# Layer-by-layer transformer trunk on one core: where the norms' sums are made and read, and in what order the mixer's small matmuls run

## The chip, the cores and the metric

One core of one Trainium2 chip runs the whole program in one launch. The metric is device microseconds (us) of one execution, the median over several. Engines are named as in the profile: PE is TensorE, PEld its weight loads, DVE VectorE, ACT ScalarE, POOL GpSimd, SP SyncE (which issues the loads).

## What is computed

```python
def reference(x, ...):                     # x: (1, 256, 1024) float32, DEPTH = 2
    for l in range(DEPTH):
        x = x + 0.5 * swiglu(rmsnorm(x, ffn1_norm[l]), ...)       # 1024 -> 2816 -> 1024
        x = x + hybrid_mixer(rmsnorm(x, mix_norm[l]), ...)
        x = x + 0.5 * swiglu(rmsnorm(x, ffn2_norm[l]), ...)
    return rmsnorm(x, final_norm)

def hybrid_mixer(h, ...):
    q_a, k_a, v_a, q_g, k_g, v_g, gate_lr, r_g = split(h @ w_in)
    attn = rmsnorm(sliding_window_attention(q_a, k_a, v_a, sinks), attn_out_norm)
    log_a = log_sigmoid(gate_lr @ gate_up + bias) / 16
    o = gla_chunked(q_g, k_g, v_g, log_a)                         # 4 chunks of 64 tokens
    gla = rmsnorm(o, gla_out_norm) * silu(r_g)
    return concat(attn, gla) @ w_out
```

The window is 128 tokens, 8 query heads share 2 key heads of 64, and the gated linear attention (GLA) has 4 heads with keys of 64 and values of 128. All weights are float32 in HBM and are read once.

## The kernel before

Activations lie transposed in SBUF: `resid` holds x as 8 tiles (k) of 128 features by 256 tokens. A float32 product is made of three fast `fp32r` matmuls: ACT rounds a weight unit to `whi` (L756), DVE makes `wlo = raw - whi` (L977), x is split in the same way into `xhi` (ACT, L770) and `xlo` (DVE, L982), and PE adds whi*xhi, whi*xlo and wlo*xhi (`three`, L358 to L360). A weight unit is 1 MB at most and goes through one of three slots (`raw`, `whi`, `wlo`); SP may load a slot again when `lo_done` tells that DVE has split it. A layer is 81 units: 33 of FFN 1, 15 of the mixer, 33 of FFN 2. Inside an FFN a hardware loop runs over groups of three units (gate, up, down); its hidden parts lie in `h_parts`.

The mixer's units are, in the order of the slots, KV, V1, Q0, Q1, QG, KG, V0, R0, R1 and six of `w_out` (`WO_K`: k = 0, 1, 2 and 3, 4, 5, 6 and 7). Units KV to R1 are projections of the normed x; k 0 to 3 of the output projection read the attention output, 4 to 7 the GLA output. Between the projections stand small float32 matmuls, each of which shows as two records on PE (a transpose as one): the scores of the 8 heads (L521), the transposes of the probabilities S (`turn_probs`, L534) and of `kend` (L587), the GLA's intra-chunk products (L604, called A here), the attention's product with V (L622 to L626), the state updates (L641), and the GLA output (L664 from A, L668 from the states `Sta`).

A norm is a seam. The last unit of a stage leaves its sum in four PSUM banks (`acc`); DVE adds them to `resid` one after the other (L1004), ACT makes `xhi` and squares `resid` (L772), POOL adds the squares up in four steps into `sqsum` (`sum_squares`, L1346), PE sums over the partitions with two matmuls against `ones` (`square_sums`, L407), and DVE works out 1/sqrt by twelve steps on two columns (`rsqrt`, L1022 to L1029). The factor is wanted along the tokens: DVE makes diagonal matrices of it in two `fp32r` parts (`diagonals`, L1034 to L1039, in `h_parts`), PE spreads them over the partitions (`spread`, L415), and DVE copies the result to `rB` (L1050). Meanwhile PE goes on with matmuls on the unnormed x, since the factor is multiplied in when a PSUM tile is read. At the seam into the mixer PE runs `up_pairs` for unit KV, `square_sums`, then unit V1, then Q0 with `spread` after its first half. At the seams into an FFN `square_sums` stands one tile later. The attention's norm and the GLA's norm go the same way with `sqsum_a` (L650, POOL too) and with 8 columns (L706).

The order of the work is that of the program text: each engine's stream is written out by hand in its own block and waits on semaphores with fixed counts. ACT's and DVE's `split_mix(i)` split unit i.

## Time and profile before

| | us |
|---|---|
| median of 3 runs | 1011.42 |
| the three runs | 1007.83, 1011.63, 1011.42 |
| the profiled execution | 1007.62 |
| its span, from the first to the last instruction | 1005.7 |
| PE busy | 972.5 (97%) |
| DVE busy | 628.4 (62%) |
| ACT busy | 457.2 (45%) |
| POOL busy | 55.8 (6%) |

The page gives busy times as a share of the span. A matmul's record is longer than the distance to the next one, since they are pipelined, so a PE that is busy all the time says only that matmuls followed one another closely; how closely is read from the number of records in a stretch. The granted clock (PEclk) is a share of 2.4 GHz; it has two levels here, 1.0 and 0.5. Layer 0 runs to about 499 us, with its mixer from 200 to 309 us; layer 1's mixer runs from 691 to 803 us.

### The profile page before, as it was taken

To read this page: it belongs to the slowest core of one execution; us is meant where nothing else is said; L and a number is where in the kernel's file an instruction comes from. 1 tells how busy PE (TensorE), PEld (TensorE's weight loads), DVE (VectorE), ACT (ScalarE), POOL (GpSimd) and SP (SyncE) were. 2 spreads that over 40 slices of the span, in tenths; PEclk is the share of its full clock that TensorE was granted. 3 is DMA by queue.
4 is the path that set the end of the run, shared out by engine and by line. 5 is a ranking of instruction groups with operands and counts; after the bars stand their busy time and mean duration, and the time that the engine had idled before them with its cause. 6 is when DMAs were issued, how large, how long until landed. Compare 5 with 4: busy or idle time off the path is not lost.

```text
span 1005.7 us, 20058 instructions
## 1 busy us (share of the span) xinstructions
PE 972.5 (97%) x8116; PEld 959.1 (95%) x8116; DVE 628.4 (62%) x743; ACT 457.2 (45%) x499; POOL 55.8 (6%) x37
## 2 busy tenths in 40 slices
PE   7999999989999999999979999998999999999996
PEld 6999999989999999999979999998998999999996
DVE  7755555667778655555665555557595785555553
ACT  5443434536645443434534343435475544343432
POOL 4000000030101000000120000003001010000000
PEclk8999999989999999999999999999998999999997
DMA  7665656544335665655446556555442556565621
GB/s 259 219 207 169 206 169 209 169 127 126 85 98 197 211 199 174 193 183 185 149 137 218 197 177 198 177 200 155 140 105 63 170 167 210 168 199 175 190 102 43
DMA packets 130621, 169.13 MB, mean 168 GB/s; under 512 B 3217, under 2 KB 116113, under 8 KB 130577
## 3 DMA queue, kind: packets, MB, share of 16 engines
q1 hardware_dynamic: 130576, 168.52, 53.0%
q8 instruction: 31, 0.51, 0.2%
q14 instruction: 14, 0.11, 0.0%
HBM read 167.46 MB, written 1.05 MB: 168 GB/s over the span
## 4 chain that ended last, share of the span: by engine, by line
PE 77%; issue 14%; DVE 4%; POOL 3%; DMA 1%; ACT 1%; SPq 0%; DVEq 0%; ACTq 0%; POOLq 0%
PE ps L358 25%; PE ps L359 25%; PE ps L360 25%; POOL sq L1346 2%; DVE xlo L982 2%; PE ps L668 1%; DVE wlo L977 1%; PE ps L664 1%; DMA raw<-in_ffn_w_gate 1%; DMA raw<-in_ffn_w_up 1%; ACT xhi L770 0%; PE ps L415 0%; POOL sqsum_a L1346 0%; PE ps L738 0%; PE ps L706 0%
## 5 line engine op out<-in xcount | busy, mean ns | idle before, releaser
L977 DVE TENSOR_TENSOR wlo<-raw,whi 128x2048 fp32r<-128x2048 f32 (+1 forms) x159 | 355.6, 2239 | 249.5 <-ACT whi L756 249.5
L358 PE MATMUL ps<-xhi,whi 128*128 128x256 f32 x1760 | 498.7, 283 | 12.8 <-DVE wlo L977 6.1
L359 PE MATMUL ps<-xlo,whi 128*128 128x256 f32 x1760 | 494.5, 281 | 0.0
L360 PE MATMUL ps<-xhi,wlo 128*128 128x256 f32 x1760 | 493.8, 281 | 0.0
L756 ACT ACTIVATE whi<-raw 128x2048 fp32r<-128x2048 f32 (+1 forms) x159 | 297.2, 1869 | 182.7 <-PE ps L360 168.9
L358 PEld LDWEIGHTS ps<-xhi,whi 128*128 128x128 f32 x1760 | 333.6, 190 | 17.2 <-issue 7.1
L359 PEld LDWEIGHTS ps<-xlo,whi 128*128 128x128 f32 x1760 | 333.0, 189 | 0.1
L360 PEld LDWEIGHTS ps<-xhi,wlo 128*128 128x128 f32 x1760 | 332.9, 189 | 0.0
L359 PE MATMUL ps<-h_parts,whi 128*128 128x256 f32 x704 | 196.1, 279 | 0.0
L360 PE MATMUL ps<-h_parts,wlo 128*128 128x256 f32 x704 | 196.1, 278 | 0.0
L358 PE MATMUL ps<-h_parts,whi 128*128 128x256 f32 x704 | 196.0, 278 | 0.0
L360 PEld LDWEIGHTS ps<-h_parts,wlo 128*128 128x128 f32 x704 | 133.6, 190 | 0.0
L358 PEld LDWEIGHTS ps<-h_parts,whi 128*128 128x128 f32 x704 | 132.2, 188 | 0.0
L359 PEld LDWEIGHTS ps<-h_parts,whi 128*128 128x128 f32 x704 | 132.1, 188 | 0.0
L1346 POOL TENSOR_TENSOR sq<-sq 128x512 f32<-128x512 f32 x21 | 42.5, 2025 | 928.6 <-ACT sq L772 625.8
L784 ACT ACTIVATE h_parts<-work 128x512 fp32r<-128x512 f32 x44 | 27.8, 632 | 145.3 <-DVE work L1066 85.0
L777 ACT ACTIVATE work<-work 128x512 f32<-128x512 f32 x44 | 27.8, 633 | 133.8 <-DVE work L1058 133.8
L1070 DVE TENSOR_TENSOR h_parts<-work,h_parts 128x512 fp32r<-128x512 f32 x44 | 30.4, 692 | 30.8 <-ACT h_parts L784 30.8
L1063 DVE TENSOR_TENSOR work<-ps,rB 128x512 f32<-128x512 f32 x44 | 30.1, 684 | 3.2 <-PE ps L360 3.2
L1066 DVE TENSOR_TENSOR work<-work 128x512 f32<-128x512 f32 x44 | 30.5, 692 | 2.1 <-ACT work L777 0.7
L1058 DVE TENSOR_TENSOR work<-ps,rB 128x512 f32<-128x512 f32 x44 | 30.2, 686 | 0.3
L982 DVE SCALAR_TENSOR_TENSOR xlo<-resid,par,xhi 128x256 fp32r<-128x256 f32 x40 | 27.6, 739 | 0.0
(138 smaller groups left out, 525.7 us busy)
## 6 DMA issues: line engine op xcount, KB each, us to landing
raw<-in_ffn_w_down SPq DMA_DIRECT2D x44, 1024.0 KB, 4.9
raw<-in_ffn_w_up SPq DMA_DIRECT2D x43, 1024.0 KB, 5.4
raw<-in_ffn_w_gate SPq DMA_DIRECT2D x42, 1024.0 KB, 5.4
raw<-in_w_in SPq DMA_DIRECT2D x12, 1024.0 KB, 5.2
raw<-in_w_in SPq DMA_DIRECT2D x8, 512.0 KB, 4.5
...
```

The source lines that it names most:

```text
L358: pe.matmul(o, w_hi, x_hi, start=start, stop=False, skip_group_check=True)
L359: pe.matmul(o, w_hi, x_lo, start=False, stop=False, skip_group_check=True)
L360: return pe.matmul(o, w_lo, x_hi, start=False, stop=stop, skip_group_check=True)
L756: nc.scalar.activation(h, r, ACT.Copy).then_inc(hi_done, 1)
L777: nc.scalar.activation(s32[:, :, :], a32[:, :, :], ACT.Silu).then_inc(silu_done, 1)
L977: nc.vector.tensor_tensor(lo, r, h.bitcast(F32), ALU.subtract).then_inc(lo_done, 1)
L982: nc.vector.scalar_tensor_tensor(out=xlo[:, m, :], in0=resid[:, m, :], scalar=gain[:, m:m + 1], in1=xhi[:, m, :].bitcast(F32), op0=ALU.mul ...
L1058: nc.vector.tensor_tensor(a32[:, :, :], tiles(bank), r_tiles(2), ALU.mult).then_inc(a_done, 1)
L1063: nc.vector.tensor_tensor(u32[:, :, :], tiles(bank), r_tiles(2), ALU.mult).then_inc(u_done, 1)
L1066: nc.vector.tensor_tensor(h32[:, :, :], s32[:, :, :], u32[:, :, :], ALU.mult).then_inc(h_done, 1)
L1070: nc.vector.tensor_tensor(hlo[hb][:, :, :], h32[:, :, :], hhi[hb][:, :, :].bitcast(F32), ALU.subtract).then_inc(hlo_done, 1)
L1346: return nc.gpsimd.tensor_tensor(o, a, b, ALU.add)
```

## The change

Of the norms: the squares are made by two ACT instructions of four tiles each (`squares`), after the next unit's split and no longer between the `xhi` of the seam; DVE adds them up in three instructions (`sum_squares`), POOL keeps the program's first and last sum alone; the mixer's `square_sums` stands after the first token tile of V1. `diagonals` is gone at all places: `spread` is now float32 matmuls of the factor's column, broadcast, against the identity, which wait for the last step of `rsqrt`; in the mixer it stands before Q0. DVE adds the attention's squares too.

Of the mixer's order: the gate's small matmuls go before Q1; each set of scores goes one projection earlier; the A products stand together ahead of the `kend` transposes and of all eight heads' transposes; R0 goes from before these to behind the state updates; in the GLA output all eight products with A come first, then the twelve with the states, in pairs of heads; the GLA's square sums stand inside R1 and its `spread` after the second `w_out` unit. The split attention output (k 0 to 3) goes to `h_parts` instead of `xhi` and `xlo`, since R1 still reads those. ACT and DVE have their splits and evictions in a new order to match.

The diff's core (declarations of semaphores and buffers, and copies that only change place, are left out, and every line stands 8 columns to the left):

```diff
+at_parts = h_parts[:, :, :, :].rearrange("p (a b) f t -> p a (b f) t", a=2)
+mixhi = [at_parts[:, 0, k, :] for k in range(4)] + [xhi[:, k, :] for k in range(4, KT)]
+mixlo = [at_parts[:, 1, k, :] for k in range(4)] + [xlo[:, k, :] for k in range(4, KT)]
...
-    def spread(o, n, a, b):
-        for part in range(2):
-            d = diag[:, part * n + a:part * n + b, :].rearrange("p a b -> p (a b)")
-            last = pe.matmul(o, ones_r[:, :], d, start=part == 0, stop=part == 1, skip_group_check=True)
+    def spread(o, call, y, n):
+        pe.wait_ge(rs_step, RS * (call + 1))
+        for i in range(n):
+            last = pe.matmul(o[i // 4][:, i % 4 * P:(i % 4 + 1) * P], y[:, i:i + 1].to_broadcast([P, P]), ident,
+                             start=True, stop=True, skip_group_check=True)
         return last
...
+    def project_tokens(i, t, outs, between=None):
...
+            if tt == 0 and between:
+                between()
...
-        square_sums(v)
-        project_tokens(M_V1, t, [ps[1][:, 0:WIDE], ps[2][:, 0:WIDE]])
+        project_tokens(M_V1, t, [ps[1][:, 0:WIDE], ps[2][:, 0:WIDE]], lambda: square_sums(v))
         pe.wait_ge(resid_up, 4 * (v + 1))
-        project(M_Q0, t, tiles(7), lambda: spread_r(v))
-        pe.wait_ge(rb_done, v + 1)
-        pe.wait_ge(lr_tok_ev, 2 * ev)
-        for tt in range(TT):
-            last = pe.transpose(ps[3][0:RANK, tt * P:(tt + 1) * P], lr_tok[:, tt, :], ident)
-        last.then_inc(lr_ps, 1)
+        spread_r(5 * l + 1, rcol)
+        def rank_tokens():
+            pe.wait_ge(rb_done, v + 1)
+            pe.wait_ge(lr_tok_ev, 2 * ev)
+            for tt in range(TT):
+                last = pe.transpose(ps[3][0:RANK, tt * P:(tt + 1) * P], lr_tok[:, tt, :], ident)
+            last.then_inc(lr_ps, 1)
+        project(M_Q0, t, tiles(7), rank_tokens)
...
+        pe.wait_ge(va_ev, ev)
+        pe.wait_ge(z_ev, 2 * ev)
+        pe.wait_ge(ke_done, ev)
+        pe.wait_ge(qe_done, ev)
+        for j in range(2):
+            for tt in range(TT):
+                for h in (2 * j, 2 * j + 1):
+                    b, c = DK * (h % 2), (2 * j + tt) * P
+                    last = pe.matmul(ps[3 + h % 2][:, c:c + P], ke[b:b + DK, j, tt * P:(tt + 1) * P],
+                                     qe[b:b + DK, j, tt * P:(tt + 1) * P],
+                                     start=True, stop=True, skip_group_check=True)
+                    if j == 1 and tt == TT - 1:
+                        last.then_inc(A_ps, 1)
         pe.wait_ge(qg_ev, ev)
-        project(M_R0, t, tiles(1))
-        pe.wait_ge(z_ev, 2 * ev)
         pe.wait_ge(kend_done, ev)
         for j in range(2):
             for tt in range(TT):
-                last = pe.transpose(ps[4][:, (2 * j + tt) * P:(2 * j + tt + 1) * P],
+                last = pe.transpose(ps[1][:, (2 * j + tt) * P:(2 * j + tt + 1) * P],
                                     kend[:, j, tt * P:(tt + 1) * P], ident)
         last.then_inc(ket_ps, 1)
...
-        for s in range(3):
+        for s in range(HEADS):
             turn_probs(s, l)
-        pe.wait_ge(ke_done, ev)
...
-                last.then_inc(A_ps, 1)
-            if h:
...
-            turn_probs(s, l)
...
+        pe.wait_ge(ket_ev, ev)
...
-        project(M_R1, t, tiles(0), attention_sums)
+        project(M_R0, t, tiles(0), attention_sums)
+        def o_tile(h):
+            return tiles(1 + h % 2)[:, h // 2, :]
+        pe.wait_ge(kg_ev, ev)
+        for h in range(GH):
+            j = h // 2
+            for tt in range(TT):
+                pe.matmul(o_tile(h)[:, tt * P:(tt + 1) * P], vg[:, tt, h * P:(h + 1) * P],
+                          AT[:, 4 * (h % 2) + 2 * j + tt, :],
+                          start=(h < 2 and tt == 0), stop=False, skip_group_check=True)
+        spread([ps[3][:, 256:512]], 5 * l + 2, rs_y, TT).then_inc(rA_ps, 1)
+        pe.wait_ge(st_done, 5 * ev)
+        for j in range(2):
+            for c in range(1, NCH):
+                for h in (2 * j, 2 * j + 1):
+                    b = DK * (h % 2)
+                    last = pe.matmul(o_tile(h)[:, c * CHUNK:(c + 1) * CHUNK], Sta[b:b + DK, c - 1, j, :],
+                                     qe[b:b + DK, j, c * CHUNK:(c + 1) * CHUNK],
+                                     start=False, stop=True, skip_group_check=True)
...
+                    if j == 1 and c == NCH - 1:
+                        last.then_inc(o_ps, 1)
+        def gla_sums():
+            pe.wait_ge(am_done, 4 * l + 2)
+            pe.wait_ge(osq_done, 2 * ev)
+            for h in range(GH):
+                for tt in range(TT):
+                    last = pe.matmul(ps[3][:, 2 * h + tt:2 * h + tt + 1],
+                                     sq[:, 4 + h, tt * P:(tt + 1) * P], ones[:, 0:1],
+                                     start=True, stop=True, skip_group_check=True)
+            last.then_inc(oss_done, 1)
...
         pe.wait_ge(rg_ev, 2 * l + 1)
-        pe.wait_ge(kg_ev, ev)
...
-        pe.wait_ge(st_done, 5 * ev)
-        for h in range(GH):
-            j, b = h // 2, DK * (h % 2)
...
-            o = tiles(1 + h % 2)[:, h // 2, :]
-            for tt in range(TT):
-                pe.matmul(o[:, tt * P:(tt + 1) * P], vg[:, tt, h * P:(h + 1) * P], AT[:, 4 * (h % 2) + 2 * j + tt, :],
-                          start=(h < 2 and tt == 0), stop=False, skip_group_check=True)
-                for c in (2 * tt, 2 * tt + 1):
-                    if c:
-                        last = pe.matmul(o[:, c * CHUNK:(c + 1) * CHUNK], Sta[b:b + DK, c - 1, j, :],
-                                         qe[b:b + DK, j, c * CHUNK:(c + 1) * CHUNK],
-                                         start=False, stop=True, skip_group_check=True)
-            if h >= 2:
-                last.then_inc(o_ps, 1)
...
-            if h == 0:
-                pe.wait_ge(adiag_done, ev)
-                spread(ps[3][:, 256:512], TT, 0, TT).then_inc(rA_ps, 1)
+        project(M_R1, t, tiles(0), gla_sums)
...
                 for m in range(KT):
                     w_hi, w_lo = weights(slot, n, D, m * P, P)
-                    last = three(acc[m // 2][:, m % 2, :], w_hi, w_lo, xhi[:, k, :], xlo[:, k, :],
+                    last = three(acc[m // 2][:, m % 2, :], w_hi, w_lo, mixhi[k], mixlo[k],
...
-                if k == 2:
-                    pe.wait_ge(o_ev, 2 * ev)
-                    pe.wait_ge(odiag_done, ev)
-                    for b in range(2):
-                        r = spread(ps[1 + b][:, :], 8, 4 * b, 4 * b + 4)
...
             last.then_inc(unit_done, 1)
...
+            if i == M_WO + 1:
+                pe.wait_ge(o_ev, 2 * ev)
+                spread([ps[1], ps[2]], 5 * l + 3, rs_y, 8).then_inc(rG_ps, 1)
...
-            nc.scalar.activation(sq[:, 2 * p:2 * p + 2, :], resid[:, 2 * p:2 * p + 2, :],
-                                 ACT.Square).then_inc(sq_done, 1)
+    def squares():
+        for half in range(2):
+            four = slice(4 * half, 4 * half + 4)
+            nc.scalar.activation(sq[:, four, :], resid[:, four, :], ACT.Square).then_inc(sq_done, 1)
...
         split_mix(2)
+        squares()
         split_mix(3)
-        act.wait_ge(rcol_done, ev)
-        v_out(M_V1, [ps[1][:, 0:UC], ps[2][:, 0:UC]])
+        act.wait_ge(rs_step, RS * (5 * l + 2))
+        act.wait_ge(unit_done, ST + 3 * t + M_V1 + 1)
         for tt in range(TT):
             nc.scalar.activation(lr_tok[:, tt, :], ps[1 + tt][:, UC:WIDE], ACT.Copy,
                                  scale=rcol[:, tt:tt + 1]).then_inc(lr_tok_ev, 1)
+        v_out(M_V1, [ps[1][:, 0:UC], ps[2][:, 0:UC]])
...
+        for s in range(4):
+            probs_out(s)
+        act.wait_ge(ket_ps, ev)
+        nc.scalar.copy(ket[:, :, :].rearrange("p a b -> p (a b)"), ps[1][:, :]).then_inc(ket_ev, 1)
         v_out(M_V0, [ps[0][:, 0:UC], ps[0][:, UC:2 * UC]])
+        for s in range(4, HEADS):
+            probs_out(s)
         split_mix(9)
-        exps(1)
-        act.wait_ge(ket_ps, ev)
-        nc.scalar.copy(ket[:, :, :].rearrange("p a b -> p (a b)"), ps[4][:, :]).then_inc(ket_ev, 1)
-        for s in range(HEADS):
-            probs_out(s)
...
-        nc.vector.tensor_copy(rs_parts[:, 0:n], rs_y[:, 0:n]).then_inc(part_step, 1)
-        dve.wait_ge(part_step, 2 * call + 1)
-        nc.vector.tensor_tensor(rs_parts[:, n:2 * n], rs_y[:, 0:n], rs_parts[:, 0:n].bitcast(F32),
-                                ALU.subtract).then_inc(part_step, 1)
-        dve.wait_ge(part_step, 2 * call + 2)
-        return nc.vector.tensor_tensor(
-            diag[:, 0:2 * n, :], ident.unsqueeze(1).to_broadcast([P, 2 * n, P]),
-            rs_parts[:, 0:2 * n].bitcast(F32).unsqueeze(2).to_broadcast([P, 2 * n, P]), ALU.mult)
-    def norm_r(v, call):
+    def norm_r(v, call, y):
         dve.wait_ge(ss_done, v + 1)
-        rsqrt(call, ps[3][:, 0:TT], TT, D)
-        diagonals(call, TT).then_inc(diag_done, 1)
+        rsqrt(call, ps[3][:, 0:TT], TT, D, y[:, 0:TT])
+    def flat(a, b):
+        return sq[:, a:b, :].rearrange("p m t -> p (m t)")
+    def sum_squares(v, steps):
+        dve.wait_ge(sq_done, 2 * v)
+        nc.vector.tensor_tensor(flat(0, 4), flat(0, 4), flat(4, 8), ALU.add).then_inc(sum_step, 1)
+        dve.wait_ge(sum_step, steps + 1)
+        nc.vector.tensor_tensor(flat(0, 2), flat(0, 2), flat(2, 4), ALU.add).then_inc(sum_step, 1)
+        dve.wait_ge(sum_step, steps + 2)
+        nc.vector.tensor_tensor(sqsum[:, :], sq[:, 0, :], sq[:, 1, :], ALU.add).then_inc(sqsum_done, 1)
...
-        norm_r(v, 5 * l + 4 * f)
+        norm_r(v, 5 * l + 4 * f, rs_y)
         split_lo(0, t + 1)
...
+        sum_squares(v, 7 * l)
         split_mix(2)
-        norm_r(v, 5 * l + 1)
-        nc.vector.tensor_copy(rcol[:, :], rs_y[:, 0:TT]).then_inc(rcol_done, 1)
+        norm_r(v, 5 * l + 1, rcol)
         split_mix(3)
         norm_b(v)
         dve.wait_ge(rb_done, v + 1)
...
         normalised(0)
-        split_mix(9)
-        normalised(1)
         for b in range(2):
             dve.wait_ge(A_ps, 2 * l + b + 1)
             dve.sem_inc(waits_met, 1)
             nc.vector.copy_predicated(AT[:, 4 * b:4 * b + 4, :], mask.unsqueeze(1).to_broadcast([P, 4, P]),
                                       ps[3 + b][:, :].rearrange("p (a t) -> p a t", a=4)).then_inc(A_ev, 1)
-        done(M_R0)
-        nc.vector.tensor_tensor(sg[:, 0:2, :], tiles(1), r_tiles(2), ALU.mult).then_inc(rg_ev, 1)
+        normalised(1)
+        split_mix(8)
...
+        dve.wait_ge(asq_done, 2 * ev)
+        nc.vector.tensor_tensor(flat(0, 2), flat(0, 2), flat(2, 4), ALU.add).then_inc(sum_step, 1)
+        dve.wait_ge(sum_step, 7 * l + 3)
+        nc.vector.tensor_tensor(sqsum_a[:, :], sq[:, 0, :], sq[:, 1, :], ALU.add).then_inc(asum_done, 1)
+        split_mix(9)
         dve.wait_ge(ass_done, ev)
-        rsqrt(5 * l + 2, ps[3][:, 0:TT], TT, 512)
-        diagonals(5 * l + 2, TT).then_inc(adiag_done, 1)
-        done(M_R1)
-        nc.vector.tensor_tensor(sg[:, 2:4, :], tiles(0), r_tiles(2), ALU.mult).then_inc(rg_ev, 1)
+        rsqrt(5 * l + 2, ps[3][:, 0:TT], TT, 512, rs_y[:, 0:TT])
+        done(M_R0)
+        nc.vector.tensor_tensor(sg[:, 0:2, :], tiles(0), r_tiles(2), ALU.mult).then_inc(rg_ev, 1)
         dve.wait_ge(rA_ps, ev)
         for b in range(2):
...
+                sum_squares(3 * l + 3, 7 * l + 5)
                 split_lo(2, t0 + TURNS)
...
+        sum_squares(3 * l + 2, 7 * l + 3)
...
-    def sum_squares(v, steps):
-        pool.wait_ge(sq_done, 4 * v - 3)
-        for p in (1, 2, 3):
-            pool.wait_ge(sq_done, 4 * v - 3 + p)
-            add(flat(0, 2), flat(0, 2), flat(2 * p, 2 * p + 2)).then_inc(pool_step, 1)
-            pool.wait_ge(pool_step, steps + p)
-        add(sqsum[:, :], sq[:, 0, :], sq[:, 1, :]).then_inc(sqsum_done, 1)
```

At the seam into the mixer this is what DVE does after the last `xlo`. Before:

```order
117 L975 REGISTER_ALU
118 L977 TENSOR_TENSOR wlo<-raw,whi 128x2176 [waits hi_done]
119 L975 REGISTER_ALU
120 L977 TENSOR_TENSOR wlo<-raw,whi 128x2x16x64 [waits hi_done]
121 L1044 REGISTER_ALU
122 L1022 TENSOR_SCALAR rs_v<-ps 128x2 [waits ss_done]
```

And with the change:

```order
111 L980 TENSOR_TENSOR wlo<-raw,whi 128x2176 [waits hi_done]
112 L1045 REGISTER_ALU
113 L1046 TENSOR_TENSOR sq<-sq 128x1024 [waits sq_done]
114 L1047 ISA
115 L1048 TENSOR_TENSOR sq<-sq 128x512 [waits sum_step]
116 L1049 REGISTER_ALU
117 L1050 TENSOR_TENSOR sqsum<-sq 128x256 [waits sum_step]
118 L978 REGISTER_ALU
119 L980 TENSOR_TENSOR wlo<-raw,whi 128x2x16x64 [waits hi_done]
120 L1037 REGISTER_ALU
121 L1026 TENSOR_SCALAR rs_v<-ps 128x2 [waits ss_done]
```

Three additions stand between the split of V1 (2176 wide) and that of Q0, and the first of them waits for ACT's squares.

In PE's stream the GLA output began like this before (one row is one matmul):

```order
1002 L664 MATMUL ps<-AT,vg 128x128 [waits st_done]
1003 L668 MATMUL ps<-qe,Sta 128x64
1004 L664 MATMUL ps<-AT,vg 128x128
1005 L668 MATMUL ps<-qe,Sta 128x64 x2
1006 L415 MATMUL ps<-h_parts,ones_r 128x256 [waits adiag_done]
1007 L415 MATMUL ps<-h_parts,ones_r 128x256
```

And is this, whole, with the change:

```order
949 L659 MATMUL ps<-AT,vg 128x128 [waits kg_ev]
950 L659 MATMUL ps<-AT,vg 128x128 x7
951 L412 ISA
952 L414 MATMUL ps<-cst,rs_y 128x128 [waits rs_step]
953 L414 MATMUL ps<-cst,rs_y 128x128
954 L664 REGISTER_ALU
955 L669 MATMUL ps<-qe,Sta 128x64 [waits st_done]
956 L669 MATMUL ps<-qe,Sta 128x64 x11
```

The two kinds of product no longer alternate, and the wait for the states comes after the products that don't need them.

## Rows read from the trace of the kernel before

**Rows 1.** The page's first part: busy time, share and instructions of each engine.

```profile
PE 972.5 (97%) x8116; PEld 959.1 (95%) x8116; DVE 628.4 (62%) x743; ACT 457.2 (45%) x499; POOL 55.8 (6%) x37
```

**Rows 2.** PE's waits over the span: us in total, times, longest.

```profile
PE ps L407 <- POOL sqsum L1346: 10.1, 3, 4.5
...
PE ps L358 <- DVE wlo L977: 6.1, 4, 3.8
...
PE ps L650 <- POOL sqsum_a L1346: 1.0, 2, 0.5
```

**Rows 3.** Timeline of POOL at the first mixer seam: start, us, instruction, idle before.

```profile
203.71 6.09 POOL L1346 TENSOR_TENSOR sq<-sq 128x512 f32<-128x512 f32 x1 [1.05 <-ACT sq L772]
209.88 0.72 POOL L1346 TENSOR_TENSOR sqsum<-sq 128x256 f32<-128x256 f32 x1
```

**Rows 4.** Timeline of DVE: `xlo` at the seams into the mixer and FFN 2; layer 1's first splits.

```profile
202.02 2.11 DVE L982 SCALAR_TENSOR_TENSOR xlo<-resid,par,xhi 128x256 fp32r<-128x256 f32 x4
...
309.76 4.67 DVE L982 SCALAR_TENSOR_TENSOR xlo<-resid,par,xhi 128x256 fp32r<-128x256 f32 x4
...
502.34 4.48 DVE L977 TENSOR_TENSOR wlo<-raw,whi 128x2048 fp32r<-128x2048 f32 x2
```

**Rows 5.** Stretches: length, each engine's busy us (instructions), granted clock, DMA, GB/s.

```profile
210.65:216.49 5.84, 5.84 (x26) 5.84 (x27) 4.30 (x17) 0.00 (x0) 0.00 (x0) 0.50 0.66 210
259.64:268.26 8.62, 8.62 (x95) 7.38 (x93) 4.92 (x14) 5.87 (x16) 0.00 (x0) 1.00 0.30 82
276.26:283.52 7.26, 7.26 (x44) 5.75 (x42) 6.25 (x9) 4.91 (x6) 0.00 (x0) 1.00 0.01 3
308.95:325.81 16.86, 15.49 (x127) 14.81 (x126) 14.97 (x24) 8.36 (x10) 4.82 (x4) 1.00 0.44 145
498.46:520.52 22.06, 16.83 (x126) 16.21 (x125) 13.54 (x24) 9.39 (x11) 9.04 (x4) 0.92 0.48 153
...
772.86:779.69 6.83, 6.83 (x28) 6.15 (x28) 3.27 (x2) 2.44 (x4) 0.00 (x0) 0.50 0.46 154
38.43:43.88 5.45, 5.45 (x50) 5.45 (x49) 2.94 (x3) 2.44 (x2) 0.00 (x0) 1.00 0.80 286
340.20:345.80 5.60, 5.60 (x50) 5.60 (x49) 3.37 (x3) 2.44 (x2) 0.00 (x0) 1.00 0.59 190
```

**Rows 6.** Timeline of PE: small matmuls, and the start of layer 1.

```profile
259.64 0.60 PE L587 MATMUL ps<-cst,kend 128*128 128x128 f32 x4
260.08 1.15 PE L534 MATMUL ps<-cst,S 128*128 128x128 f32 x9
261.15 0.72 PE L604 MATMUL ps<-qe,ke 64*128 64x128 f32 x8
...
265.70 0.27 PE L626 MATMUL ps<-PT,va 128*64 128x128 f32 x1
...
267.84 0.27 PE L624 MATMUL ps<-PT,va 128*64 128x128 f32 x1
...
276.26 0.38 PE L664 MATMUL ps<-AT,vg 128*128 128x128 f32 x2
276.57 0.43 PE L668 MATMUL ps<-qe,Sta 64*128 64x64 f32 x2
...
516.07 0.38 PE L358 MATMUL ps<-xhi,whi 128*128 128x256 f32 x1 [3.81 <-DVE wlo L977]
```

**Rows 7.** Groups of one shape: count, busy us, mean ns, idle before.

```profile
L977 DVE TENSOR_TENSOR wlo<-raw,whi 128x1024 fp32r<-128x1024 f32 x8 | 9.8, 1219 | 0.0
L1027 DVE SCALAR_TENSOR_TENSOR rs_a<-rs_a,rs_v 128x2 f32<-128x2 f32 x27 | 4.3, 161 | 0.9
L1156 DVE TENSOR_TENSOR bd<-bb 128x256 f32<-128x256 f32 x4 | 1.5, 422 | 0.1
```

**Rows 8.** Timeline of ACT: the seam's last `xhi`, and the split behind it.

```profile
202.13 0.91 ACT L770 ACTIVATE xhi<-resid,par 128x256 fp32r<-128x256 f32 x2 [1.00 <-DVE resid L1004]
...
203.47 1.90 ACT L756 ACTIVATE whi<-raw 128x2048 fp32r<-128x2048 f32 x1
```

170 lines of the change are left out of this document (62 added, 108 removed).

## The prediction

> **What bounds the kernel now.** I read the page's first part, then PE's waits, then the stretches at the seams, then the timelines inside them. PE is busy for 972.5 us of a span of 1005.7 [rows 1], so the program is PE's stream of matmuls, and a change can only take away PE's waits, make the same matmuls follow one another faster, or undo half clock. PE's waits [rows 2] are few: 10.1 us for POOL's `sqsum` in three places (the longest 4.5, twice, at the mixer's seams, and 1.08 at the seam between the layers), 6.1 for DVE's `wlo` (3.8 of it at one place), 1.0 for `sqsum_a`. Everything on the other engines beside these is hidden.
>
> At the mixer's seam POOL's third addition (512 wide) takes 6.09 us, the 256 wide one behind it 0.72 [rows 3]. DVE's four `xlo` take 2.11 there, but 4.67 at FFN 2's seam [rows 4], where POOL is busy for 4.82 us [rows 5]. So POOL's and DVE's operations, both of which read two tensors of SBUF, hold each other up; alone, POOL's 512-wide one would be near twice 0.72.
>
> Behind the wait at the mixer's seam comes a stretch at half clock (granted 0.50): PE, at 1.2 instead of 2.4 GHz, works in it from 210.65 to 216.49 [rows 5], 5.84 us, half of which is lost, 2.92. A second cause is the small matmuls. The V products follow one another in 0.054 us (40 records from 265.70 to 267.84), since two tiles of 64 columns run at once; the four `kend` transposes on the whole array take 0.11 each (0.44 from 259.64 to 260.08) [rows 6]. The GLA output takes 7.26 us for 44 records [rows 5], 0.165 each, because it alternates two forms: from the first pair at 276.26 the next form starts 0.31 later [rows 6], where two records of one form take 0.22.
>
> **The change, part by part.** The sum is made against the profiled execution, 1007.6 (3.8 below the median of the runs, 1011.4; one half-clock stretch more costs about 3.4, see below, so I take the gap for that and do not add it).
>
> *The mixer's seam.* DVE gets three additions between V1's split and Q0's. A 1024-wide two-tensor operation takes 1.22, a 256-wide one 0.42 [rows 7], so 512 take 0.7 and the three 2.3. Working layer 0: ACT's last `xhi` ends at 203.0 before; without the squares between them it ends at 202.05. Then come a split of 1.90 [rows 8] to 203.95 and two squares of half that width, about 1.0 each, to 205.9. DVE's last `xlo` ends at 202.9, V1's split (2.3, as each of the two at 502.34 [rows 4]) at 205.2; DVE then waits for ACT, and adds until 208.3. Behind its wait stands Q0's split, done at 210.6, which PE wants at 212.5. PE runs `up_pairs` until 205.9, where it stops today, and V1's first tile (24 matmuls of 272 columns, 0.117 x 272 / 256 = 0.125 each) until 208.9. So the sums are there 0.6 before PE asks for them. The wait of 4.5 goes, and with it the half clock that follows it: 4.5 + 2.9 = 7.4 a layer, **-14.9** in two.
>
> *The seams into FFN 2 and between the layers.* In 308.95 to 325.81 PE needs 120 matmuls of 0.117 (5.60 for 48 in FFN 2) and 0.6 for the sums and the spread, 14.6 of 16.86 [rows 5]; 2.2 are waits, for POOL or for an `xlo` that POOL slows. I take 1.9 of it, **-3.8** in two. The Trainium skill ("SBUF — State Buffer", who interferes with whom) has a VectorE operation with two SBUF inputs and a GpSimd one that reads SBUF lock each other out for a whole instruction. By that rule the four `xlo` here would go back to 2.11 from 4.67, 2.6 a seam and no more than the waits allow, so the term would be -4.4 and the sum 983.4; without the rule, were `xlo` slow for a cause of its own, nothing would go here and the sum be 987.8. The trace agrees with the rule as far as 4.67 beside POOL and 2.11 ahead of it go. Between the layers (22.06 us [rows 5]) 3.81 [rows 6] are a wait that the profile puts down to `wlo`, though the splits of that unit ended at 506.8 [rows 4], 5.4 us before PE stopped; I read it as the turn of PE's outer loop, which stays with its half clock (0.92 on the mean of 22 us). What is left is the 1.1 for POOL and smaller ones: **-1.5**.
>
> *The GLA output.* Sixteen records of A products at 0.11 are 1.76; the spread's four 0.44; twelve state products in pairs of heads (64 rows each, side by side as the V products) 24 x 0.054 = 1.3; two changes of form 0.4. Together 3.95 for 7.26: **-6.6** in two layers. From below: if the pairs do not run side by side, 1.3 a layer are lost. In layer 1 this output stands in a stretch of 6.83 at clock 0.50 [rows 5], which costs 3.4; without the alternation I expect none: **-3.4**.
>
> *The attention's sums* are on DVE, behind the states, before R0 is half done, and R1's split behind them is needed a unit later, so the wait of 0.5 a layer [rows 2] goes: **-1.0**.
>
> *The transposes and A products.* The stretch 259.64 to 268.26 takes 8.62 [rows 5]. It loses four changes of form at 0.1 to 0.2, but the cover that R0 gave it is gone: the softmax of heads 3 to 7 has to be ready at V0's end. ACT's copies of P (8 of 384 columns; two of 256 take 0.91 [rows 8]) take 3.7 against 2.9 for the transposes (three at 0.12 a head), so PE waits for PSUM banks toward the end. I cost it at nothing, between -0.6 (only the changes of form) and +1.5 a layer (the 0.8, and as much for its hand-overs).
>
> *The float32 spreads.* Two fp32r matmuls of 256 columns become four records at 0.11 with two changes of form: 0.24 becomes 0.6, +0.35 at six seams, +2.1. The GLA's goes from four matmuls of 512 columns (0.24 each, twice a 256-wide one, 0.94 in all) to 16 records at 0.11 and a change of form, 1.9: +1.0 a layer, +2.0. Together **+4.1**. `diagonals` leaves DVE, three operations a norm, which were hidden behind Q0's first half or V1; with `spread` now before Q0, rsqrt is on the path instead.
>
> *New waits.* rsqrt is twelve steps of about 0.2 (0.161 busy [rows 7] and the semaphore): 2.35. DVE reaches it at 210.6, behind Q0's split, and ends at 212.95, where PE comes to `spread` at 212.5: 0.5 a layer. `gla_sums` in the middle of R1 waits for ACT's squares of the GLA output, which now start 10 us nearer to it: 0.35 a layer. Behind both stand only matmuls that nothing else is late for. Together **+1.7**. Some more changes of form in the mixer, **+0.4**, and for fourteen hand-overs between engines that I cannot see 0.1 each, **+1.4**.
>
> Sum: -14.9 - 3.8 - 1.5 - 6.6 - 3.4 - 1.0 + 4.1 + 1.7 + 0.4 + 1.4 = -23.6, so **984.0**. R0's new place adds no matmul, and SP's loads see the slots freed in the same order; at the seams they lead by several us (DMA busy 0.3 to 0.5 of these stretches [rows 5]).
>
> One thing nobody edited: 48 down matmuls of an FFN take 5.45 in FFN 1 and 5.60 in FFN 2 [rows 5]. The instructions are the same and only their place in the program differs, and that moves by some rows. Over 1056 such matmuls in the two FFN 2 (0.003 each) this is 3.3 us to win, or as many to lose in FFN 1. The forecast's own range goes down from 984.0 by that 3.3, by 1.4 (no hand-overs), 1.7 (no new waits), 1.2 (the transposes at their best) and 1.4 (a spread with no change of form), to 975, and up by 3.3, by 2.6 (pairs not side by side) and 3.0 (the transposes at their worst), to 993.
>
> **The rivals.** *The clock still falls.* Before, the same GLA output kept full clock in layer 0 and stood at half in layer 1 (772.86 to 779.69 [rows 5]), with the same instructions, so a fall is not decided by the program's text alone. One or two stretches at 3.4: 987.4 or 990.8. The Trainium skill ("TensorE: Matmul & The Clock Gate") has a clock gate that is not tied to the kernel's start; by that rule the place of a fall varies from run to run, which the trace bears out as far as two layers with one program differ. Against a fall: behind the seam PE no longer idles. Chance 0.14.
>
> *The sums come too late again.* The margin of 0.6 rests on ACT: a split of 1.90 and two squares between its last `xhi` and the additions [rows 8]. If ACT is 1.5 late, PE waits at V1's half, and the clock falls as before. The most is the whole of the first term back, 14.9: 998.9. Chance 0.10.
>
> *No change:* waits move (to rsqrt, to P's copies and to the late W splits) and the time stays within 0.5% of 1011.4, about what a measurement of this kernel can tell from none. The terms above would have to be refilled by 20 us, with only four new places to wait: 0.04.
>
> *Slower: PE's inner loop pays for its turn.* The outer loop's turn costs 3.81 [rows 6] with all data there. The mixer's code before FFN 2 grows shorter by 14 rows, so FFN 2's hardware loop lies elsewhere. If its turn came to cost the same, 18 passes (9 in each layer) would be 69 us, 1053; the change is slower from 9 of 18 passes on. No pass of an inner loop shows such a wait before. The Trainium skill ("Runtime: NRT & Kernel Launch", instruction fetch) has instructions fetched ahead in order, and a taken jump to one not held waits for its fetch; the 3.81 agrees, and no run here shows a wait of the inner loop. Chance 0.05.
>
> **How the numbers follow.** Forecast 0.67, clock 0.14, late sums 0.10, no change 0.04, slower 0.05. Faster by over 0.5% are the first three, 0.91. The range from 975 to 999 holds the forecast, the clock's cases and nearly all of the late sums.
>
> **What would show it.** Right: no PE wait for `sqsum`, granted clock 1.0 from 200 to 220 us, a GLA output of 4 us, POOL nearly idle and FFN 2's four `xlo` near 2.1. Wrong: a wait at L407's successor or at `spread` above 1 us, half clock in a mixer, transposes over 10 us from V0's end to the V products' end, or FFN 2's 48 down matmuls far from 5.6.

## The result, and the profile after

| | before | after |
|---|---|---|
| median, us | 1009.62 (4 runs) | 973.38 (4 runs) |
| lowest to highest | 1005.07 to 1011.63 | 971.09 to 977.13 |
| the profiled execution | 1007.62 | 971.30 |

The ratio is 0.9651, with a 95% interval of 0.9599 to 0.9703. The forecast was 984.0, with 975 to 999: the sign is right, the gain is larger than the range allowed.

The first two parts of the page of the kernel after (busy time by engine, and the granted clock in 40 slices):

```profile
PE 950.8 (98%) x8156; PEld 942.1 (97%) x8156; DVE 617.2 (64%) x729; ACT 456.6 (47%) x489; POOL 11.4 (1%) x13
...
PEclk9999999999999999999999999999999999999998
```

PE has 40 matmul records more than in [rows 1] and is busy 22 us less; POOL works only at the start and in the last norm. PE's waits over the span of the kernel after (us in total, times, longest):

```profile
PE ps L357 <- DVE wlo L996: 5.2, 2, 2.8
PE ps L414 <- DVE rs_y L1033: 2.4, 1, 2.4
PE ps L357 <- issue: 1.6, 1, 1.6
PE ps L535 <- ACT PT L875: 1.1, 2, 0.6
PE ps L716 <- DVE ones L1288: 1.1, 1, 1.1
PE ps L535 <- DVE S L1192: 0.6, 2, 0.3
PE ps L681 <- ACT sq L909: 0.5, 2, 0.3
PE ps L414 <- DVE rcol L1033: 0.4, 2, 0.2
```

Against [rows 2]: the 10.1 for `sqsum` and the 1.0 for `sqsum_a` are gone. New are four waits of the mixer: for ACT's copies of P (`PT`), for DVE's probabilities (`S`), for the GLA's squares and for the mixer's rsqrt (L414, `rcol`), 2.6 us in both layers together. The 3.8 at the start of layer 1 is now 1.6, and the profile puts it down to "issue": it shows nothing that PE waited for.

The stretches that answer to [rows 5] (start and end, length, busy us of PE, PEld, DVE, ACT, POOL with instructions, granted clock, DMA, GB/s):

```profile
201.20:213.67 12.47, 12.32 (x102) 12.10 (x100) 11.26 (x24) 6.96 (x8) 0.00 (x0) 1.00 0.39 113
248.02:257.02 9.00, 8.13 (x94) 6.79 (x93) 6.50 (x18) 7.60 (x21) 0.00 (x0) 1.00 0.02 2
264.36:268.17 3.81, 3.81 (x47) 3.62 (x45) 2.07 (x5) 3.44 (x4) 0.00 (x0) 1.00 0.15 61
...
485.59:502.01 16.42, 14.84 (x126) 14.64 (x125) 13.49 (x24) 10.34 (x11) 0.00 (x0) 1.00 0.45 150
...
37.25:42.90 5.65, 5.65 (x50) 5.65 (x49) 3.11 (x4) 2.44 (x2) 0.00 (x0) 1.00 0.79 278
323.93:329.38 5.45, 5.45 (x51) 5.45 (x50) 2.98 (x3) 2.40 (x2) 0.00 (x0) 1.00 0.81 286
```

They are: the seam into the mixer up to `spread` (12.5 at full clock); A products, transposes and V products (9.0, where it was 8.6); the GLA output (3.8, where it was 7.3); the seam between the layers (16.4, where 22.1 stood); and 48 down matmuls of layer 0, first of FFN 1 (5.65), then of FFN 2 (5.45). Before it was 5.45 and 5.60, the other way round. Below, "pace" means this: whether an FFN's 48 down matmuls take 5.45 or 5.65 us.

DVE at the mixer's seam and at FFN 2's, after (start, us, instruction, idle before):

```profile
203.60 2.41 DVE L980 TENSOR_TENSOR wlo<-raw,whi 128x2176 fp32r<-128x2176 f32 x1
206.77 1.23 DVE L1046 TENSOR_TENSOR sq<-sq 128x1024 f32<-128x1024 f32 x1 [0.76 <-ACT sq L771]
208.03 0.69 DVE L1048 TENSOR_TENSOR sq<-sq 128x512 f32<-128x512 f32 x1
208.75 0.42 DVE L1050 TENSOR_TENSOR sqsum<-sq 128x256 f32<-128x256 f32 x1
...
301.23 1.66 DVE L985 SCALAR_TENSOR_TENSOR xlo<-resid,par,xhi 128x256 fp32r<-128x256 f32 x4
```

The sums are there at 209.17, and PE asks at 209.88: 0.7 us to spare, where 0.6 was forecast. The four `xlo` take 1.66 where they took 4.67 beside POOL [rows 4].

Cut at the ends of the same FFN steps, the 36.3 us between the two profiled executions lie like this. From the start to the end of layer 0's FFN 1 +1.1; layer 0's mixer with the seams 140.1 to 128.2, -11.9; FFN 2 158.3 to 156.2, -2.1; the seam between the layers with the first step behind it 36.2 to 30.8, -5.4; layer 1's FFN 1 156.2 and 156.2; its mixer 143.4 to 128.2, -15.2; its FFN 2 158.3 to 156.2, -2.1; the end -0.7.

### The profile page after: what moved, and what is told of

Read it like the earlier page. It is cut to its first block, busy times and chain, and to the rows that moved or that the text cites. A ratio compares the mean times of both kernels' runs of the same rounds, so it can differ in the third digit from the quotient of the medians.

```text
span 969.5 us, 20036 instructions
## 1 busy us (share of the span) xinstructions
PE 950.8 (98%) x8156; PEld 942.1 (97%) x8156; DVE 617.2 (64%) x729; ACT 456.6 (47%) x489; POOL 11.4 (1%) x13
## 4 chain that ended last, share of the span: by engine, by line
issue 97%; DMA 1%; POOL 1%; PE 0%; DVE 0%; SPq 0%; POOLq 0%; DVEq 0%
DMA raw<-in_ffn_w_gate 1%; POOL sq L1349 0%; PE ps L736 0%; DVE sq L1341 0%; SPq L284 0%; POOLq L98 0%; SPq L287 0%; PE ps L414 0%; POOL sq L1358 0%; POOL sqsum L1349 0%; DVEq L98 0%; DVE rs_y L1033 0%; DVE rs_a L1031 0%; DVE rs_a L1030 0%; SPq L286 0%
## 5 line engine op out<-in xcount | busy, mean ns | idle before, releaser
L357 PE MATMUL ps<-xhi,whi 128*128 128x256 f32 x1696 | 477.2, 281 | 6.8 <-DVE wlo L996 5.2
L358 PE MATMUL ps<-xlo,whi 128*128 128x256 f32 x1696 | 475.0, 280 | 0.0
L359 PE MATMUL ps<-xhi,wlo 128*128 128x256 f32 x1696 | 474.0, 279 | 0.0
L357 PEld LDWEIGHTS ps<-xhi,whi 128*128 128x128 f32 x1696 | 319.3, 188 | 9.3 <-issue 5.4
L359 PEld LDWEIGHTS ps<-xhi,wlo 128*128 128x128 f32 x1696 | 318.4, 188 | 0.0
L357 PE MATMUL ps<-h_parts,whi 128*128 128x256 f32 x768 | 213.2, 278 | 0.0
L358 PE MATMUL ps<-h_parts,whi 128*128 128x256 f32 x768 | 213.1, 277 | 0.0
L359 PE MATMUL ps<-h_parts,wlo 128*128 128x256 f32 x768 | 213.0, 277 | 0.0
L357 PEld LDWEIGHTS ps<-h_parts,whi 128*128 128x128 f32 x768 | 144.2, 188 | 0.0
L358 PEld LDWEIGHTS ps<-h_parts,whi 128*128 128x128 f32 x768 | 144.1, 188 | 0.0
L1074 DVE TENSOR_TENSOR h_parts<-work,h_parts 128x512 fp32r<-128x512 f32 x44 | 30.4, 691 | 30.8 <-ACT h_parts L782 30.8
L1007 DVE SCALAR_TENSOR_TENSOR resid<-ps,resid 128x512 f32<-128x512 f32 x24 | 16.6, 690 | 11.5 <-PE ps L359 11.5
L764 ACT ACTIVATE xhi<-resid,par 128x256 fp32r<-128x256 f32 x40 | 18.2, 502 | 7.8 <-DVE resid L1007 7.7
```

The lines of the kernel that those rows point to most:

```text
L357: pe.matmul(o, w_hi, x_hi, start=start, stop=False, skip_group_check=True)
L358: pe.matmul(o, w_hi, x_lo, start=False, stop=False, skip_group_check=True)
L359: return pe.matmul(o, w_lo, x_hi, start=False, stop=stop, skip_group_check=True)
L764: nc.scalar.activation(xhi[:, m, :], resid[:, m, :], ACT.Copy, scale=gain[:, m:m + 1]).then_inc(xhi_done, 1)
L1074: nc.vector.tensor_tensor(hlo[hb][:, :, :], h32[:, :, :], hhi[hb][:, :, :].bitcast(F32), ALU.subtract).then_inc(hlo_done, 1)
```

## Experiments: what the sums are worth

The kernel before was timed again beside each group of runs: medians 1003.28 (first four), 1006.80 (next four) and 1006.56 (last three), of 13 runs each. Its runs reach from 996.5 to 1014.7, so the ratio, with its 95% interval behind it, and the traces say more than differences of medians.

**The new sums alone** (`before_new_sums`):

```diff
 # the kernel before
+    squares()                      # two of four tiles, after the next split; none between the xhi
...
+    sum_squares(v, 6 * l)          # on DVE, three additions, in place of POOL's four
...
-    square_sums(v)
-    project_tokens(M_V1, t, ...)
+    project_tokens(M_V1, t, ..., lambda: square_sums(v))
```

> The kernel before with one part of the change alone: squares in two instructions after the next split, the norms' sums on DVE, and in the mixer read after V1's first tile; the order of the mixer's small matmuls, the fp32r spreads and the attention's sums on POOL stay. Theory A (the sums are nearly all of it): 24 to 27 us less than before, 976 to 982 where before is 1003 to 1007, and the order of the mixer is worth 5 to 8 us. Rival B (the parts share one gain, the clock): under 18 us less. At the turn of the loop between the layers: 3.8 us idle as before, if that idle time follows from where the code lies; 1.6 or less, if it came from the wait for the sums ahead of it.

984.64 (982.33 to 987.70), ratio 0.9803 (0.9729 to 0.9878), profiled 983.92: 23.7 less than the profiled execution before, but 22.2 less by the medians and 19.8 by the ratio. That is between the two theories, nearer to A; the interval of the ratio (12 to 27 us) can't choose. PE's waits of this run:

```profile
PE ps L359 <- issue: 2.1, 1, 2.1
...
PE ps L652 <- POOL sqsum_a L1368: 1.0, 2, 0.5
PE ps L416 <- DVE h_parts L1047: 0.9, 1, 0.9
```

No wait for `sqsum` is left. The turn of the loop (PE's jump from the end of layer 0 back to the start of the loop's body) shows 2.1, between the two values that were expected. What also shows is half clock in both layers, from the middle of the GLA output on:

```profile
274.90:281.70 6.80, 6.80 (x29) 6.12 (x29) 2.98 (x2) 2.26 (x4) 0.00 (x0) 0.50 0.45 155
...
752.70:759.50 6.80, 6.80 (x29) 6.34 (x29) 2.84 (x2) 2.12 (x4) 0.00 (x0) 0.50 0.43 154
```

Before, this stretch lost its clock in layer 1 alone, so the half clock in layer 0, 3.4 us of loss, is held against the new sums here.

**POOL instead of DVE, all else as in the change** (`pool_sums_late`):

```diff
 # the kernel after
-                sum_squares(v, 7 * l)            # and the two other calls in DVE's block
+            with pool.Fori(0, DEPTH) as l:       # the same three additions, by gpsimd
+                sum_squares(3 * l + 1, 6 * l)
...
```

> The changed kernel with the inner norms' three additions on POOL instead of DVE; PE reads the sums where the change reads them. Theory A (the engine matters): POOL needs some 5 us for them even alone (0.72 for 256 wide), and more beside DVE's splits, so they are ready 2 to 6 us after PE asks inside V1; with a returned half clock that is 3 to 9 us in each mixer and 1 to 3 at each of the three other seams: 985 to 1000 against 973. Rival B (only the place of the reading matters): PE waits under 0.5 us at each seam and the time stays within 3 us of 973.

998.43 (994.82 to 999.91), ratio 0.9940 (0.9905 to 0.9974): nearly all of the gain is gone. POOL at FFN 2's seam, and PE's wait over the span:

```profile
309.59 4.84 POOL L1347 TENSOR_TENSOR sq<-sq 128x1024 f32<-128x1024 f32 x2 [98.95 <-ACT sq L772]
314.51 0.72 POOL L1347 TENSOR_TENSOR sqsum<-sq 128x256 f32<-128x256 f32 x1
```

```profile
PE ps L407 <- POOL sqsum L1347: 13.3, 5, 2.7
```

POOL needs 5.6 us where DVE needs 2.4 (beside DVE's splits; a 512-wide addition of POOL with nothing beside it, near this run's end, took 1.29), and PE waits 2.7 at each of the five seams. Half clock stands behind four of the five waits (3.4 us, 6.8 at the seam between the layers) and at the GLA output of both layers, 23.9 us in all, half of it lost: 13.3 and 11.9 make up 25 of the 27 us by which this profiled execution (998.65) is longer than the change's. Theory A. Its detail was wrong: the mixers' seams wait no longer than the others. And one wait, at layer 0's FFN 2 seam, brought no half clock: the stretch from 311 to 323 us shows 1.00.

**DVE, but read ahead of V1** (`read_before_v1`):

```diff
 # the kernel after
-    project_tokens(M_V1, t, ..., lambda: square_sums(v))
+    square_sums(v)
+    project_tokens(M_V1, t, ...)
```

> The changed kernel with the mixer's square sums ahead of V1, as before the change, the additions still on DVE. DVE's sums were ready about 208.3 to 209 and PE would ask at 206.9. Theory A: PE waits 1.5 to 2.5 us in each mixer, too short for the clock to fall; rsqrt starts no later, so nothing else moves: 976 to 979. Rival B: the clock falls behind that wait as it did before the change: 2.9 more in each mixer, 982 to 985.

980.48 (977.27 to 982.16), ratio 0.9784 (0.9702 to 0.9865). The first two square sums of the mixer, and the stretch behind them:

```profile
206.48 0.49 PE L406 MATMUL ps<-ones,sqsum 128*128 128x1 f32 x3 [2.27 <-DVE sqsum L1051]
```

```profile
207.00:210.40 3.40, 3.40 (x16) 3.40 (x16) 3.09 (x11) 0.00 (x0) 0.00 (x0) 0.50 0.43 120
```

Half clock came behind a wait of 2.27 in both layers: 2.27 + 1.7 each, 8 in all. Theory A had the wait right, and Rival B the clock, though the stretch was 3.4 us long where the kernel before had 5.84 behind its wait, and the time lies between the two ranges. So the faster additions alone do not undo the wait at the mixer's seam: the later reading has its part.

**Only the reading moved, in the kernel before** (`before_read_late`): the same edit as above, the other way round, with POOL and ACT untouched:

```diff
 # the kernel before
-    square_sums(v)
-    project_tokens(M_V1, t, ...)
+    project_tokens(M_V1, t, ..., lambda: square_sums(v))
```

> The kernel before with nothing changed but the place where PE reads the mixer's sums: after V1's first tile; squares, POOL's additions and all else as before. POOL had them ready at 210.6 and PE would now ask at 209. Theory A (the long wait brings half clock): the wait falls from 4.5 to 1.5 us in each mixer and the half clock behind it goes or shrinks to one stretch of 3.4: 3 to 6 us less in each, 995 to 1001 where before is 1003 to 1007. Rival B (POOL and DVE slow each other whatever PE does, and V1's matmuls wait for a split that is late instead): under 3 us less in all.

996.30 (993.09 to 1001.22), ratio 0.9910 (0.9880 to 0.9939). Theory A. Its waits, in part:

```profile
PE ps L358 <- issue: 2.8, 1, 2.8
PE ps L407 <- POOL sqsum L1347: 2.7, 3, 1.0
```

The wait for the sums in the mixer is 0.9 in place of 4.5, with a new one of 0.4 for V1's split ahead of it (Rival B's wait, but small), and the seam keeps full clock. The half clock behind the GLA output got longer here, 10.2 us in layer 0 and 3.4 in layer 1 where the kernel before had 6.8 in layer 1 alone, so 3.4 us of the gain at the seams don't show in this execution's total. Moving one call, without a new engine, gives 9 us by the ratio and 10 by the medians, of the 36.

## Experiments: the GLA output and the rest of the mixer

**The old order inside the changed kernel** (`gla_alternating`):

```diff
 # the kernel after
-    pe.wait_ge(st_done, 5 * ev)    # behind the eight products with A and the spread
+    pe.wait_ge(st_done, 5 * ev)    # ahead of all
+    for h in range(GH):            # as before: A, state, A, state, state; spread behind h == 0
```

> The changed kernel with the GLA output's two kinds of products alternating head by head as before. Theory A (changes of form and no pairs cost it): the output takes 7.3 us again instead of 3.8, +3.5 in each layer, 980 to 981; with one fall of the clock as in layer 1 before, 984. Rival B (what was slow there was the wait for the states, which now are ready earlier): under 1 us more in all.

979.01 (977.78 to 984.36), ratio 0.9778 (0.9690 to 0.9866). The output of layer 0:

```profile
265.08:272.60 7.52, 7.52 (x47) 6.01 (x45) 4.68 (x8) 5.45 (x7) 0.00 (x0) 1.00 0.20 66
```

7.5 for 3.8 of the same matmuls, 3.7 a layer; PE is busy all through, so no wait for the states hides in it. Theory A without the fall of the clock: in this place the alternating order kept 1.0 in both layers.

**New sums and new GLA order, nothing else** (`before_sums_gla`):

```diff
 # the kernel with the new sums
-    for h in range(GH):            # A, state, A, state, state
+    for h in range(GH):            # A, A; the spread behind, still fp32r
+    for j in range(2):             # then the states, c by c, in pairs of heads
```

> The kernel before with the new sums (as in the run of them alone) and the new order inside the GLA output: all products with A first, then the states' in pairs of heads, in its old place behind R1. Theory A (alternating forms cost time and let the clock fall): the output takes 3.8 to 4.0 us instead of 7.3, and the half clock that stood in both layers at that place (6.8 us each, behind 274.9 and 752.7) is gone in both: 7 us by the order and up to 6.8 by the clock less than with the new sums alone, 971 to 978. Rival B (the clock falls there for its surroundings, the state updates, square sums and transposes): 7 us less and no more, 977 to 979, with half clock still in one or both layers.

972.26 (970.76 to 975.73), ratio 0.9656 (0.9611 to 0.9701); the whole change, timed again beside it, 972.17 (970.73 to 976.17), ratio 0.9673 (0.9624 to 0.9723). Two of the change's parts give all of it, as far as the runs can tell. The output's stretch in this run:

```profile
269.70:274.24 4.54, 3.67 (x44) 3.40 (x43) 3.56 (x7) 3.68 (x5) 0.00 (x0) 1.00 0.02 5
746.50:751.10 4.60, 3.73 (x45) 3.46 (x43) 3.58 (x8) 3.75 (x5) 0.00 (x0) 1.00 0.01 4
```

Theory A: the order is worth 3.6 a layer, and in this execution the half clock behind it is gone in both. 0.87 of the 4.5 is a new wait, named in PE's waits:

```profile
PE ps L359 <- DVE xlo L1275: 1.7, 2, 0.9
...
PE ps L652 <- POOL sqsum_a L1369: 1.0, 2, 0.5
```

The split attention output is late now that the GLA output, 3.6 us shorter, no longer covers it. The full change removes this wait and that for `sqsum_a` (2.7 in both layers): R1 stands there instead. It pays with 0.4 at the transposes, 0.8 for the float32 spread of the GLA, 0.1 to 0.3 at each seam's spread, and waits of 0.2 and 0.3. These cancel within what the runs can tell.

Whether half clock comes in or behind the GLA output is only in part a matter of this order. With the alternating order it came in five of eight layers (four traces: one layer before, two of `before_new_sums`, two of `before_read_late`, none of `gla_alternating`), for 3.4 to 10.2 us. With all the changed mixer it came in five of sixteen layers (eight traces: one layer each of `read_before_v1`, `pool_layer_seam` and `after_shift_208`, two of `pool_sums_late`), each time for 3.4 us, and with the grouped output alone in none of two. So few traces can't tell how much rarer the new order makes it; they show that it is no cure.

**ACT's copies of V0 moved back** (`v0_copy_last`), a version meant to beat both:

```diff
 # the kernel after, ACT
-    v_out(M_V0, ...)
     for s in range(4, HEADS):
         probs_out(s)
+    v_out(M_V0, ...)
```

> The changed kernel with ACT's two copies of V0's result behind all eight copies of P instead of between the fourth and fifth. Theory A (these copies hold up the transposes): PE's wait of 0.55 at the last transposes falls below 0.1, 0.4 to 0.5 us less in each layer, which the total can't tell from none: 970 to 976. Rival B: the wait moves to the state updates, which need V0's result, and nothing is won.

971.41 (967.19 to 973.61), ratio 0.9674 (0.9603 to 0.9745). L535's wait for ACT (1.1 after) is not among this run's waits, and nothing new is: theory A. The profiled 967.19 is the lowest of all, but in time it can't be told from the change.

## Experiments: the turn of the loop between the layers

**That seam's sums on POOL** (`pool_layer_seam`): the edit of the run with POOL, for one seam:

```diff
 # the kernel after
-                        sum_squares(3 * l + 3, 7 * l + 5)      # DVE
+                    sum_squares(3 * l + 3, 2 * l)              # POOL, the same additions
```

> The changed kernel with the sums of the one seam between the layers on POOL. There the change won 5.4 us where I had forecast 1.2. Theory A (instruction fetch behind a wait): PE's sequencer runs ahead of the array and asks for the instructions behind the loop's turn before the array is there; a wait of the array's stream for the sums takes that lead away. Then the wait at the sums of 2 to 4 us comes with an idle time at the turn that grows from 1.6 to about 3.8, and half clock returns: 5 to 9 us more in all, 979 to 982. Rival B (the turn's cost follows from where the code lies): the idle time at the turn stays at 1.6 and the total grows by the wait for the sums alone, 2 to 4 us.

976.34 (975.00 to 977.19), ratio 0.9740 (0.9659 to 0.9820). The only idle time of PE that the timeline lists between 496 and 504 is this:

```profile
496.99 0.61 PE L407 MATMUL ps<-ones,sqsum 128*128 128x1 f32 x4 [2.74 <-POOL sqsum L1349]
```

A wait of 2.74, a stretch of half clock from 498.0, and no idle time listed at the turn. `pool_sums_late` has none there either. Both theories fall; I read it so, that the fetch of the instructions was all but done before PE, delayed by half clock, came to the turn. The times of the fetch below bear this out.

**The code moved by 208 and by 160 instructions**:

```diff
 # the kernel after, PE, ahead of first_group()
+            for _ in range(208):            # 160 in the other
+                pe.sem_inc(waits_met, 1)
```

> The changed kernel with 208 semaphore increments ahead of PE's first matmuls, while it waits for the first weights anyway: all later code lies 208 instructions further on, which puts the turn of the outer loop about where it lay in the kernel before, as counted from the last fetch of instructions (28 matmuls behind it, 52 in the changed kernel). Theory A (place in the code decides what the turn costs): idle time of 3.0 to 3.8 us at the turn instead of 1.58, with half clock behind it, 4 us more in all, 977. Rival B (not the place): 1.3 to 1.6 us at the turn and 971 to 975.

> The same with 160 increments: the turn lies only a few matmuls behind a fetch. Theory A: an idle time at the turn that differs from both 1.58 and that of the shift by 208 by over 0.5 us; if a fetch in flight holds up the next, the largest of the three, over 3.8. Rival B: 1.3 to 1.6 again. In both, FFN pieces of 48 matmuls take 5.45 or 5.65, and which of the two, in which FFN, does not follow from the shift.

996.30 (995.57 to 1000.76) and 992.30 (988.55 to 993.52). Both totals lie about 20 us above the change's and say nothing on the turn, since the increments were not hidden at the start: 208 of them kept PE idle for 29.12 us, 0.14 each, where the first group began. That was an error of the design. The idle times at the turn can be read all the same, of the shift by 208 first, then by 160:

```profile
523.24 0.38 PE L357 MATMUL ps<-xhi,whi 128*128 128x256 f32 x1 [2.22 <-issue]
```

```profile
514.94 0.38 PE L357 MATMUL ps<-xhi,whi 128*128 128x256 f32 x1 [1.37 <-issue]
...
519.40 0.39 PE L358 MATMUL ps<-xlo,whi 128*128 128x256 f32 x1 [2.31 <-issue]
```

Same instructions, other addresses: 1.58, then 2.22, then 1.37 and a second stop of 2.31 behind it. For the shift by 208 neither theory has the size; for that by 160 the first stop is Rival B's, and the second was in neither.

That instructions are fetched there is in the DMA part of the profile. The kernel before, from 512.30 to 516.00, inside its idle time, and the kernel after, from 495.8 to 497.5, ahead of its own:

```profile
q8 instruction: 1, 0.02, 1.8%
```

```profile
q8 instruction: 1, 0.02, 4.3%
```

One packet of instructions each. The traces have its start and end to the hundredth of a us (all times in us from the span's start):

| run | PE reads the sums | packet starts | packet ends | PE goes on behind the turn | idle at the turn |
|---|---|---|---|---|---|
| before | 508.82 | 513.40 | 514.45 | 516.07 | 3.81 |
| `before_read_late` | 507.11 | 510.74 | 511.85 | 513.43 | 2.78 |
| `before_new_sums` | 498.25 | 500.52 | 502.15 | 503.82 | 2.13 |
| after | 494.07 | 496.32 | 497.50 | 499.09 | 1.58 |
| `after_shift_208` | 517.58 | 519.91 | 521.60 | 523.24 | 2.22 |
| `after_shift_160` | 510.14 | 512.41 | 513.36 | 514.94 | 1.37 |
| `pool_layer_seam` | 496.99 | 499.55 | 500.48 | 502.06 | none listed |

In each row PE goes on 1.6 us behind the packet's end (1.57 to 1.67, and so in all other traces but that of `pool_sums_late`, where PE at half clock doesn't stop at all). So I take the idle time at the turn for a wait for this fetch, though the profile puts it down to `wlo` in one trace and to "issue" in the others. With the sums on DVE the packet starts 2.2 to 2.3 us behind the reading of the sums, in nine traces of nine; what is left to differ is how long the packet took, from 0.93 to 1.69 us. In `after_shift_208` it took 1.69 and started as another packet of instructions ended: that is most of the 0.6 between 2.22 and 1.58, and as far as that the place in the code matters. The second stop of the shift by 160 has a packet of its own, from 516.89 to 518.15, with PE going on at 519.40. Why the packet starts later with the sums on POOL (4.6, 3.6, 3.4 and 2.6 us behind the reading) stays open: `before_read_late` waits for its sums ahead of the turn nearly as long as the kernel before (0.98 and 1.08) and has hardly other code on PE. The Trainium skill ("Runtime: NRT & Kernel Launch", instruction fetch) has a jump out of the held instructions wait for a fetch; these rows agree.

## Experiment: the same program twice

> The changed kernel, nothing edited. In the traces so far the 48 down matmuls of an FFN step take 5.45 or 5.65 us, the same from the first to the last step of one FFN, and this changed between kernels whose instructions up to there are the same. Theory A (a state of the run, not of the program): of the four FFNs (slow, fast, fast, fast in the first trace) at least one stands at the other pace now, each worth 2.3 us, or a stretch of half clock of 3.4 us stands where none was. Rival B (the program decides): the same pattern again, and a time within 1 us of 971.3 for the profiled execution.

Profiled at 970.73, and the step that took 5.65 in layer 0's FFN 1 takes 5.45 here:

```profile
38.45:43.90 5.45, 5.45 (x50) 5.45 (x49) 2.94 (x3) 2.44 (x2) 0.00 (x0) 1.00 0.89 313
```

Theory A, though the time is also within Rival B's 1 us of 971.3. One FFN at the other pace is 528 matmuls of 0.0043 us, 2.3 us. It is gained here, and most of it is lost again at the start: a stretch of half clock stands at 19.4, behind PE's last wait for the first weights, and costs 1.7; the first trace had it at 10.0, ahead of such a wait (2.8 us, to 17.9). The two executions belong to different groups of runs, perhaps on different chips; but `gla_alternating` and `pool_layer_seam`, both on one chip and with the same instructions of PE up to there, have layer 0's FFN 1 at 5.65 and 5.45 too. In the traces of this study each of the four FFNs was seen at either pace, from none slow (`before_read_late`) to three (`before_sums_gla`, `pool_sums_late`).

## Why the prediction was right, and where it was wrong

Forecast -23.6 on the profiled execution, measured -36.3.

| term, both layers | forecast | in the traces |
|---|---|---|
| mixer's seam with its spread and wait | -13.2 | -14.4 |
| FFN 2 seams with their spread | -3.1 | -4.3 |
| seam between the layers, with its spread | -1.2 | -5.4 |
| GLA output | -6.6 | -6.9 |
| clock behind it in layer 1 | -3.4 | -3.4 |
| transposes | 0 | +0.8 |
| GLA's spread | +2.0 | +1.5 |
| attention's sums | -1.0 | -1.0 |
| wait for the GLA's squares | +0.7 | +0.5 |
| hand-overs and changes of form | +1.8 | none found |
| pace of the down matmuls | 0 | -2.3 |
| start and end, with one spread | +0.4 | -1.8 |

The measured terms add up to 36.7, 0.4 too much. The mixer's seam, from the end of FFN 1 to behind the spread and without the half of Q0 that stood ahead of it before, went from 19.8 to 12.8 us in layer 0 and from 20.1 to 12.8 in layer 1. FFN 2's is the 120 matmuls ahead of the spread, in 16.85 and then in 14.58 us. The pace was lost in one FFN and won in two. The large terms were the right ones and nearly of the right size, and the time worked out for DVE's sums (208.3, PE at 208.9) is what the trace shows 0.9 later on both sides, since layer 0's FFN 1 ended 1.1 later. One of them was luck: the -3.4 for the clock in layer 1 rested on "without the alternation I expect none", and five of sixteen layers with the new order had half clock there after all.

**The step that failed** is the sentence that the turn of the outer loop "stays with its half clock". 3.81 became 1.58, and the half clock behind it went: 2.2 + 1.7 of the 4.2 us missing there. I took the longest idle time of that seam as fixed because no edit touched it. The runs show 0 to 3.8 us for the same turn: it lasts until 1.6 us behind the end of an instruction fetch, and that fetch started 4.6 us behind the reading of the sums before and 2.2 after.

**Second**, costs were charged that did not come: 1.8 for hand-overs and changes of form that no row had shown, two waits that are smaller (0.16 and 0.21 for 0.5, 0.27 for 0.35), and seam spreads at 0.36 to 0.47 us for the 0.6 assumed. The term for FFN 2's seams was mis-sized too. The sum that let the four `xlo` go back to 2.11 came out nearer: it had -4.4, -3.8 was taken, and -4.5 was measured without the spread, with the `xlo` at 1.66. Together some 4.4 us.

**Third**, the pace, +3.3 or -3.3 in the range, was taken as a matter of where the code lies. It changes from run to run, and gave -2.3 here by chance. Start and end gave 2.2 more than forecast: the trace before had stretches of half clock at 8.3 and at 18.5, this one has one at 10.0 alone.

**The rivals.** The clock that still falls: not in the first trace, but in five of the sixteen layers that were traced with the change's order, counted above; part of the spread from 971 to 977 may be this. The sums that come too late did not happen, with 0.7 us to spare; `read_before_v1` and `pool_sums_late` show what it would have cost. The inner loop never paid for its turn: nowhere behind the start does PE wait inside an FFN's loop.
